# A fused two-block layer on one core: root table loaded first, first weight chunk in row halves, token copies moved behind the scalings

## The reference, cut to what matters

```python
def _rms(x, w, eps=1e-6):
    xf = x.astype(jnp.float32)
    y = xf * lax.rsqrt(jnp.mean(xf * xf, axis=-1, keepdims=True) + eps)
    return (y * w.astype(jnp.float32)).astype(x.dtype)
...
    h = jnp.concatenate([meta, x], axis=1)
...
        n = _rms(h, norm_mix_w[l])
        z = n @ w_in[l]
        q, k, v, glu, g_att, g_conv = jnp.split(z, splits, axis=-1)
```

## Time and profile before

| | |
|---|---|
| Median of 3 runs | 1598.64 us (1598.61 to 1600.5) |
| The profiled execution's own time | 1598.73 us |
| Its span, first to last instruction | 1597.0 us |
| TensorE matmuls, busy | 1545.4 us, 97% of the span |
| VectorE, busy | 1126.3 us, 71% |
| ScalarE, busy | 661.3 us, 41% |
| Mean granted TensorE clock | 0.992 |

### The profile page before, as it was taken

The page is one execution under the profiler, slowest core; times in us unless marked ns, Lnnn a source line. Parts: engine busy times, 40 slices in busy tenths (PEclk is TensorE's granted clock), DMA queues, the critical chain, the costliest instruction groups (busy, mean ns, idle before and its releaser), DMA issues.

```text
span 1597.0 us, 25517 instructions
## 1 busy us (share of the span) xinstructions
PE 1545.4 (97%) x10044; PEld 1377.8 (86%) x10044; DVE 1126.3 (71%) x1586; ACT 661.3 (41%) x1035; POOL 11.4 (1%) x26
## 2 busy tenths in 40 slices
PE   7998999999899999999999999989899999999998
PEld 7997899999899999999988888868778788888887
DVE  5889878888656478777774558787746987877213
ACT  5232465546562343433333335733536233333112
POOL 0000000000000000000000010000000000000000
PEclk9999999999999999999999999999999999999999
DMA  6232211122122333233223343222122333323221
GB/s 173 80 86 73 80 54 53 54 75 59 53 80 80 94 92 102 81 94 90 80 65 108 90 119 78 67 53 66 54 69 65 104 103 83 105 81 116 95 90 53
DMA packets 235294, 131.63 MB, mean 82 GB/s; under 512 B 20920, under 2 KB 228676, under 8 KB 235220
## 3 DMA queue, kind: packets, MB, share of 16 engines
q1 hardware_dynamic: 234836, 130.40, 28.9%
q0 software_dynamic: 384, 0.20, 0.0%
HBM read 128.48 MB, written 2.10 MB: 82 GB/s over the span
## 4 chain that ended last, share of the span: by engine, by line
PE 82%; DVE 10%; ACT 5%; issue 2%; DMA 0%; DVEq 0%; ACTq 0%
PE psP L660 28%; PE psS L660 21%; PE psP L725 8%; DVE conv L2020 4%; PE psS L1328 4%; PE psP L1328 4%; PE psP L682 4%; PE psP L1019 3%; DVE wl L1920 1%; PE psP L1196 1%; ACT wh L1380 1%; PE psS L1196 1%; ACT prob L1481 1%; PE psP L875 1%; PE psP L788 1%
## 5 line engine op out<-in xcount | busy, mean ns | idle before, releaser
L1920 DVE TENSOR_TENSOR wl<-raw,wh 128x2048 fp32r<-128x2048 f32 x124 | 284.1, 2291 | 170.6 <-ACT wh L1380 168.8
L660 PE MATMUL psP<-xh,wh 128*128 128x264 f32 (+2 forms) x1312 | 324.6, 312 | 9.2 <-ACT qkv L1470 5.6
L660 PE MATMUL psP<-xl,wh 128*128 128x264 f32 (+2 forms) x1312 | 318.9, 308 | 0.0
L660 PE MATMUL psP<-xh,wl 128*128 128x264 f32 (+2 forms) x1312 | 318.5, 308 | 0.0
L1380 ACT ACTIVATE wh<-raw 128x2048 fp32r<-128x2048 f32 x124 | 236.9, 1910 | 160.3 <-PE psS L1328 74.3
L660 PEld LDWEIGHTS psP<-xh,wh 128*128 128x128 f32 x1312 | 213.0, 190 | 27.0 <-ACT qkv L1470 6.9
L660 PEld LDWEIGHTS psP<-xl,wh 128*128 128x128 f32 x1312 | 213.7, 189 | 11.9 <-issue 0.2
L660 PEld LDWEIGHTS psP<-xh,wl 128*128 128x128 f32 x1312 | 213.3, 190 | 11.9
L660 PE MATMUL psS<-xh,wh 128*128 128x258 f32 (+2 forms) x752 | 183.6, 308 | 0.4 <-DVE hT L1949 0.4
L660 PE MATMUL psS<-xh,wl 128*128 128x258 f32 (+2 forms) x752 | 182.7, 307 | 0.0
L660 PE MATMUL psS<-xl,wh 128*128 128x258 f32 (+2 forms) x752 | 182.3, 306 | 0.0
(11 more groups left out here) (456 smaller groups left out, 2435.7 us busy)
## 6 DMA issues: line engine op xcount, KB each, us to landing
raw<-in_w_in_dram SPq DMA_DIRECT2D x76, 512.0 KB, 4.9
raw<-in_w_up_dram SPq DMA_DIRECT2D x44, 512.0 KB, 5.0
raw<-in_ffn_up_dram SPq DMA_DIRECT2D x44, 512.0 KB, 4.9
raw<-in_ffn_down_dram SPq DMA_DIRECT2D x22, 512.0 KB, 4.0
raw<-in_w_out_dram SPq DMA_DIRECT2D x16, 512.0 KB, 4.7
raw<-in_w_down_dram SPq DMA_DIRECT2D x16, 384.0 KB, 3.6
raw<-in_w_down_dram SPq DMA_DIRECT2D x16, 320.0 KB, 4.0
raw<-in_w_conv_out_dram SPq DMA_DIRECT2D x8, 512.0 KB, 4.6
```

The source lines that it names most:

```text
L660: ins = mm(ps[0:rows, a, 0:nn], W[:, s, half, k, 0:rows], Y[:, k, c0 + a * nn:c0 + (a + 1) * nn], start=(k == 0 and p == 0), stop=(k == KT ...
L1920: V.tensor_tensor(wl[:, n % 2], raw[:, n % 2], wh[:, n % 2].bitcast(f32), ALU.subtract).then_inc(s_lo, 1)
```

## The change

1. ScalarE's program begins with a load of the table that holds the root (`preload_act_table`), ahead of every wait. The two table loads that stood at the first copy and at the first root are gone, since the copy and the square are taken with this table too.
2. Chunk 0 is transferred in four pieces of 256 KB: rows 0 to 511 of both column halves first, with a semaphore of their own (`s_r0`), then rows 512 to 1023. `first_hi(0)` waits for the first two pieces alone.
3. VectorE's copies of raw tokens 0 and 1 stand behind all four scalings and behind the meta tokens' rest, and ahead of `first_lo(0)`.

```diff
+        s_r0 = sem("first_half_loaded")
...
             G = 3 * D
-            pair(w_in, 0, None, 0, G, G + D)
+            for j, s in enumerate((s_r0, s_raw[0])):
+                k = slice(4 * j, 4 * j + 4)
+                for half in range(2):
+                    c = G + half * D
+                    sp.dma_start(raw[:, 0, half, k], kp(w_in)[:, k, c:c + 128]).then_inc(s, 16)
             pair(w_in, 1, None, 0, G + 128, G + D + 128)
...
+            nc.scalar.preload_act_table(ACT.Sqrt)
             act.wait_ge(s_id, 5)
             flat = sq[:].rearrange("p a b -> p (a b)")[:, 0:D]
             act.wait_ge(s_wt, 1)
...
             def first_hi(j):
-                act.wait_ge(s_raw[0], 32)
+                act.wait_ge(s_raw[0] if j else s_r0, 32)
                 fn(wh[:, 0, :, 4 * j:4 * j + 4], raw[:, 0, :, 4 * j:4 * j + 4], ACT.Copy).then_inc(s_hi if j else s_h0, 1)
...
                     V.tensor_tensor(mw[:], halves(128), vmix[:].rearrange("p (k o) -> p k o", o=1).to_broadcast([128, KT, NM]),
                                     ALU.mult).then_inc(s_mx, 1)
-                elif t > 1:
-                    keep_tokens(t - 2, psP[t - 2])
             dve.wait_ge(s_ms, 1)
             V.tensor_tensor(xl[:, :, 0:NM], mw[:], xh[:, :, 0:NM].bitcast(f32), ALU.subtract).then_inc(s_ms, 1)
+            for t in range(2):
+                keep_tokens(t, psP[t])
             first_lo(0)
```

## The result

The changed kernel takes 1604.72 us (median of 16 runs, 1600.62 to 1605.71), the kernel before 1599.91 us (16 runs, 1598.61 to 1605.06). The ratio is 1.0021, with a 95% interval of 1.0011 to 1.0030: slower by 0.2%, where 1597.9 us and a gain of 0.05% were forecast. The time also lies outside the stated range, 1596.2 to 1601.3.

A forecast was written before the change was run, and what follows sets the result against it. TensorE's stream of products bounds the kernel, its start held by VectorE. Fourth scaling 1.86 us earlier less one copy of 1.13 gives 0.73, row halves 0: 1597.9 us, range 1596.2 to 1601.3.

The forecast's parts named there:

- What bounds the kernel: Whole kernel: TensorE 82% of the span, a stream of products; VectorE's instructions hold its start at 17.19 us.
- the order of VectorE's chain: Head: fourth scaling 11.30, meta rest, two copies, two rests, product 16.46; the new order of copies gives nothing.
- The table load: ScalarE's head: one load goes, one is hidden; squares from about 5.5, fourth scaling 1.86 us earlier, at 11.3.
- The row halves: Chunk 0's transfer: `first_hi(0)` starts at 11.3, but the split is worth 0; two more issues at 0.43 us each.
- TensorE's clock: Ahead of chunk 0's first product: idle time grows to 2.8 us, no fall assumed; fallen clock 1601.3 us, chance 0.11.
- The sum: Behind the first product to the end: the 0.73 us gain passes through, median 1597.9 us.
- this rival: Later low clock stretches: one half as long or half as long again, 1.7 us, 1596.2 or 1599.6; chance 0.23.
- The base: Kernel before: median taken as 1598.64 us, the profiled execution 0.09 above it.

The follow-up runs named there:

- much idle work at the head: Changed kernel plus idle identity transposes on TensorE at the head (13 behind the transposed weight row, 8 ahead of the normed transposes, 10 behind the first three): 1601.91 us.
- late idle work: Changed kernel plus idle matmuls on TensorE in its three long idle times (near 153, 430 and 1047 us), head as in the changed kernel: 1599.12 us.
- little idle work: Changed kernel plus five idle transposes on TensorE ahead of the normed transposes and six behind the first three of them: 1600.50 us.

## Why the prediction was wrong

- **What bounds the kernel, and the order of VectorE's chain: right.** 5.16 us from the fourth scaling to the product were worked out and measured, and without the copies' new place the product was to start at about 16.0 and started at 15.97.
- **The table load: right in kind, 0.4 us too large in the profile after.** The squares wait for the landings now; there they came at 5.80, not 5.5, and the squares were 1.41 us apart. The fourth scaling is at 11.73, not 11.3, and the product at 16.89, not 16.46: 0.30 us gained instead of 0.73. That was a later landing in this one execution: in the three other profiles with this order on VectorE and ScalarE (little and much idle work at the head, late idle work) the tokens are squared from 5.37 to 5.50 on, the fourth scaling is at 11.17 to 11.32 and the product at 16.33 to 16.48. (The 1.87 us of the meta transposes are 1.89 by their rows; nothing hangs on it.)
- **The row halves: right** for this kernel, worth 0 (0.9999 alone, and no wait for them in the profile after). The two more issues were put at 0.43 us each; the four took 4.08 us together, and nothing waited for it.
- **TensorE's clock: this step failed first.** I took no fall, by the 2.8 us of idle time ahead of the product against falls seen after 3.6. I looked for a fall only and at one gap only, and took from one profile that the clock would be up by the normed transposes. In the profile after the clock had not even risen, and the product began at 1.2 GHz (2.98 us instead of 1.70), which with the rest up to 118 cost 1.30 us: from 0.30 ahead to 1.00 behind. With the table load alone it did fall, after 2.09 us idle, as long as the 2.1 and less than the 2.8 that I had held to be safe; with the copies alone it stayed up through 2.82 us. The Trainium skill, page "TensorE: Matmul & The Clock Gate", section "Part 4: PE-mode transpose", says that transposes do not count as activity. The traces keep contradicting it: the clock rises during transposes alone in several kernels here (by 6.95 with thirteen idle ones), and eleven idle transposes gave 4.2 us back.
- **The sum: this step cost most.** "I let the 0.73 us pass through to the end" holds where the later low stretches stay (table and halves, 1.05 us at 117 and 1.1 at the end). In most executions of the changed kernel they do not (14 of 16 by their times). Of the profile's 6.2 us the head made 1.05, and 5.15 came behind 433: longer stretches at 433 and 1051, and a new one at 1132. I had named this rival and sized it at one stretch, 1.7 us; three changed together in the profile, and 4.8 us were measured for them in the kernel with the halves alone.
- **The base.** I took three runs, 1598.61 to 1600.5, and one profile for the time of the kernel before. They were all of the lower group. In a third to a half of its executions it is 4 to 5 us slower. So the forecast of the median was from the start that of one group.

**Shown:** most of the loss lies in longer and added stretches at 1.2 GHz, and what TensorE does in its idle time at the head changes how often an execution is in the upper group. The same code with idle transposes and no other difference went from 2 of 16 to 8 of 12 lower, and with the copies alone from none of 12 to 6 of 12. They ran on other chips than the kernels without the idle transposes, but the kernel before was lower there in 15 of 29, no more often than in 11 of 16 and 21 of 35. **Not shown:** how. A low clock at the head isn't needed for it: with the copies alone, and in the profiled execution with little idle work, the clock was up at the product and the later stretches were long. In all five profiles of the copies alone the clock was up at the product and TensorE only 0.4 us late until 117, and still all five lost 3.6 to 4.7 us behind it. A shift of 0.4 us alone can't be it, as the same kernel with idle transposes has its product just as late. I supposed that in the missing executions the clock falls at the head, as it does with the table load alone; no profile of such an execution was obtained.

## What to carry to other kernels

When an edit shifts work at the head, ask what it does to TensorE's idle times, not only to its start: time gained on VectorE can be lost to a low clock at the product, and small differences there went with 4 to 5 us at idle times up to a millisecond later. Read the rate from the matmuls' durations as well as from the granted clock, and look at the spread of many runs before taking one profile as the kernel: if there are two groups, a change can act by moving executions between them. Where TensorE must idle some microseconds, idle matmuls into free PSUM can pay (0.21% faster here on the kernel before, 0.28% with the two good parts of the change and idle work at the head), but look for the new gap that each may leave behind it.

## What the runs showed of the hardware that was not expected

- The granted clock reads 1.00 near the start of an execution although TensorE is at 1.2 GHz: 13 matmuls in 2.9 us in the window from 16.9 to 19.8 of the changed kernel, where the first 12 take 2.98 us against 1.70 in the kernel before.
- Two executions that reach 433 us within 0.02 us of each other (of the kernel before and of the one with the halves alone) differ by 4.8 us through the clock alone: the idle times are the same to 0.01 us (3.65 and 3.66, 2.08 and 2.09), and the low stretches at them 6.8 or 10.2 us long, or there or not.
- At 1130.6 TensorE kept 2.4 GHz behind an idle time of 2.08 us in the profile before, and an idle time of 2.08 or 2.09 went with a fall in the two others. At the head the clock fell after 2.09 us (table load alone) and 2.34 us (much idle work), and stayed up through 2.82 us (copies alone). So no single length of idle time separates a fall from none.
- Executions of the same code differ in when the clock rises at the head: with the copies alone the 12 normed transposes took 1.53 us in three profiles and 2.59 and 2.70 in two.
